# A streaming encoder layer with a product-key lookup beside it: stage barriers replaced by waits for producers, other paces, choices at other slots

## What is computed

```python
h = modulate(x, sh1, sc1)                       # layer norm, scale and shift from a vector c
gq, gk, gv, glr, gog, sq, sk, sv, mg_a, mg_b = split_cols(h @ w_in)
o_gla, s_fin = gla_recurrence(q, k, v, log_a, gla_s0)             # branch A, 4 heads
o_sb = stick_breaking(sbq, k_all, v_all, ...)                     # branch B, 16 heads of 64
mix = (sigmoid(mg_a) * branch_a + sigmoid(mg_b) * branch_b) @ w_o
x = layer_norm(DN_ALPHA * x + g1 * mix, ln1_w, ln1_b)
h2 = modulate(x, sh2, sc2)
# PEER: per token and head, the 16 best of 128 x 128 experts by two lists of 128 scores
sc, ix = lax.top_k(s, PEER_TOPK)
top, pos = lax.top_k(cand, PEER_TOPK)
g = softmax(top)
act = gelu(einsum('nhkd,nd->nhk', peer_u[eid], h2))
f = einsum('nhk,nhkd->nd', g * act, peer_v[eid])
x = layer_norm(DN_ALPHA * x + g2 * f, ln2_w, ln2_b)
```

## The kernel before

| stage | norm | stick | gla | mix | res | select |
|---|---|---|---|---|---|---|
| group 0, before and changed | 0 | 0 | 0 | 0 | 0 | 12 |
| group 1, before | 20 | 157 | 236 | 308 | 331 | 370 |
| group 1, changed | 15 | 168 | 243 | 311 | 333 | 370 |
| group 2, before | 378 | 551 | 626 | 695 | 717 | 754 |
| group 2, changed | 372 | 548 | 624 | 694 | 716 | 754 |

## Time and profile before

### The profile page before, as it was taken

One profiled execution on the slowest core, in us unless ns is written; L12 is line 12 of the kernel. 1 busy time (PEld: TensorE's weight loads), 2 busy tenths in 40 slices (PEclk: granted clock), 3 DMA queues, 4 the chain that ended last, 5 costly groups with the idle time before them and its releaser, 6 DMA issues.

```text
span 4522.3 us, 46382 instructions
## 1 busy us (share of the span) xinstructions
PE 3384.7 (75%) x16026; PEld 1667.0 (37%) x16026; DVE 2746.2 (61%) x6580; ACT 924.9 (20%) x1992; POOL 2407.8 (53%) x2375
## 2 busy tenths in 40 slices
PE   7988989878879989696899899798753433434355
PEld 4555755445536544253444356443320000000000
DVE  3343420689877864777776878655687676664420
ACT  3543210114432210013444523200100000000000
POOL 0000000134467756455877777655567777777776
PEclk9998999989989999898999999899865555555556
DMA  8774453478799999999999999999999999999998
GB/s 310 259 275 180 175 170 98 156 293 267 268 339 394 412 401 416 386 409 360 387 393 399 343 382 393 396 400 389 386 376 420 419 406 420 419 404 420 420 407 360
DMA packets 422694, 1572.17 MB, mean 348 GB/s; under 512 B 47720, under 2 KB 63464, under 8 KB 411328
## 3 DMA queue, kind: packets, MB, share of 16 engines
q0 software_dynamic: 340384, 1289.90, 72.6%
q1 hardware_dynamic: 78448, 271.38, 16.0%
...
...
## 4 chain that ended last, share of the span: by engine, by line
PE 44%; POOL 16%; DVE 16%; DMA 14%; issue 8%; ACT 2%; SPq 0%; ACTq 0%; DVEq 0%; POOLq 0%
PE wide L1847 8%; POOL peer_u_ring L2459 7%; DMA peer_v_ring<-in_peer_v,expertsT 6%; POOL peer_v_ring L2469 5%; PE bank L2526 5%; PE wide L2164 5%; DVE peer_u_ring L2632 4%; PE wide L1415 4%; POOL w_ring L2469 3%; PE wide L768 3%; DMA peer_u_ring<-in_peer_u,experts 3%; PE wide L1403 3%; PE bank L1847 2%; PE wide L831 2%; DMA w_ring<-in_peer_v,expertsT 2%
## 5 line engine op out<-in xcount | busy, mean ns | idle before, releaser
L2459 POOL DMA_INDIRECT peer_u_ring<-in_peer_u,experts x1098 | 1130.5, 1030 | 593.9 <-issue 287.5
L2632 DVE SCALAR_TENSOR_TENSOR peer_u_ring<-peer_u_ring,wide 128x1024 f32<-128x1024 f32 x682 | 821.3, 1217 | 560.1 <-DMA peer_u_ring<-in_peer_u,experts 541.7
L2469 POOL DMA_INDIRECT peer_v_ring<-in_peer_v,expertsT x840 | 880.6, 1048 | 478.1 <-PE bank L2526 254.5
L2526 PE MATMUL bank<-peer_v_ring,peer_lone 128*32 128x512 f32 x3360 | 559.4, 744 | 430.7 <-DMA peer_v_ring<-in_peer_v,expertsT 383.0
L2632 DVE SCALAR_TENSOR_TENSOR peer_u_ring<-peer_u_ring,peer_h 128x1024 f32<-128x1024 f32 x416 | 499.8, 1219 | 25.3 <-SPq L286 15.7
L2526 PE MATMUL bank<-w_ring,peer_lone 128*32 128x512 f32 x1056 | 249.9, 1035 | 348.1 <-DMA w_ring<-in_peer_v,expertsT 346.1
L2526 PEld LDWEIGHTS bank<-peer_v_ring,peer_lone 128*32 128x32 f32 x3360 | 78.2, 118 | 760.0 <-issue 712.9
L2469 POOL DMA_INDIRECT w_ring<-in_peer_v,expertsT x264 | 251.2, 951 | 84.4 <-issue 68.6
L2164 PE MATMUL wide<-mT,w_ring 128*128 128x384 f32 x768 | 266.3, 498 | 10.8 <-DMA w_ring<-in_weights 7.9
L768 PE MATMUL wide<-hT,w_ring 128*128 128x384 f32 x768 | 264.6, 491 | 6.1 <-DVE sb_hide L2746 3.1
L1415 PE MATMUL wide<-w_ring,hT 128*128 128x256 f32 x1152 | 263.8, 387 | 3.1 <-DVE gla_v L1741 3.1
...
## 6 DMA issues: line engine op xcount, KB each, us to landing
...
mod_w<-in_w_ada SPq DMA_DIRECT2D x15, 1024.0 KB, 11.1
...
```

The source lines that it names most:

```text
L2459: pool.indirect_dma_start(buffer, None, K.A["peer_u"], bass.IndirectOffsetOnAxis(ap=K.ids_of[:, j % CHOSEN, k:k + 1], axis=0)).then_inc(lo ...
L2469: pool.indirect_dma_start(buffer, None, K.A["peer_v"], bass.IndirectOffsetOnAxis(ap=K.ids_of_turned[:, j % CHOSEN, t:t + 1], axis=0)).then ...
L2526: last = pe.matmul(self.F.psum[strip:strip + 32, :], self.lone[:, mark - at:mark - at + 32], self.buffer("v", m)[0][:, c * HALF:(c + 1) * ...
L2632: dve.scalar_tensor_tensor(u, u, 1.0, h2, ALU.mult, ALU.mult, accum_out=self.dots[:, j % 2, k:k + 1]).then_inc(self.dot_done, 1)
```

## The change

`start` becomes `after`, which waits only for the engines that are named, and of those only PE and DVE report the end of a stage (`ended`). In nearly all places nothing is named, and waits for the very thing that is needed stand instead: PSUM banks kept, `mix.added` chunk by chunk, stores landed (`sequence_stored`, `outputs_stored`, `rows_stored`) on the engine that overwrites. SP waits for PE where it waited for all. POOL waits for the h2 rows and for PE's and DVE's ends.

The rows of x for the next group's norm go to a place of their own (`norm_x_behind`), are loaded in select and scaled there by DVE, between heads 2 to 5 of the choice (`scale_rows`, `more`). ACT takes the exponentials of the last two heads in the next norm and stick. Mix begins with the four chunks that need only `hT`, and `MIX_ORDER` orders the weights so. Res takes its eight weight chunks one by one.

In `paces` a slot of the first tile (s under 128) weighs `LONE_U` = 0.8 of another, and norm's units go from 10 to 3 for groups 1 and 2. The choice of a tile that is not a group's first begins 100 slots into the tile ahead of it, one head in every 12 slots, so that it ends 65 slots into its own tile; before it began 10 slots into the tile ahead (30 for tile 1, with 10 slots a head). Its ids are turned at slot 68 of its own tile, not 9. The h2 of the dots is read from PSUM in mix and res and in the tail, and from SBUF in norm and select too.

```diff
+LONE_U = 0.8
+MIX_ORDER = [(0, 0), (0, 1), (1, 0), (1, 1), (0, 2), (0, 3), (1, 2), (1, 3)] + [(j, m) for j in range(2, KC) for m in range(4)]
...
-    def start(self, e, G, name):
+    def after(self, e, G, name, *who):
...
         if at:
-            e.wait_ge(self.stage_done, 4 * at)
+            for w in who:
+                e.wait_ge(self.ended[w], at)
...
-    def end(self, e):
-        e.drain().then_inc(self.stage_done, 1)
+    def end(self, e, who):
+        e.drain().then_inc(self.ended[who], 1)
...
-        units += [10.0] * 2
+        units += [3.0 if g.n else 10.0] * 2
...
+        weights = [LONE_U if s < SLOTS else 1.0 for s in range(before, to)]
+        total, done, at, spent = sum(units[here:stop]), 0.0, before, 0.0
         for w in units[here:stop]:
             done += w
-            out.append(int(before + (to - before) * done / total))
+            while at < to and spent + weights[at - before] <= sum(weights) * done / total + 1e-6:
+                spent += weights[at - before]
+                at += 1
+            out.append(at)
...
+    def scale_rows(self, dve, G):
+        n, x = self.steps_before(G), self.x_of(G)
+        stats, mv, v, y, t = self.small_of(G)
+        for i in range(G.nt):
+            dve.wait_ge(self.x_in[i], 16 * sum(i < g.nt for g in GROUPS[:G.n + 1]))
+            for c in range(2):
+                dve.bn_stats(stats[:, i, c, :], x[:, i, c * HALF:(c + 1) * HALF]).then_inc(self.steps, 1)
+            dve.wait_ge(self.steps, n + 2)
+            dve.bn_aggr(mv[:, i, :], stats[:, i, :, :]).then_inc(self.steps, 1)
+            n += 3
+            yield
+        dve.wait_ge(self.steps, n)
+        n = rstd_steps(dve, self.steps, n, mv[:, 0:G.nt, 1], 1.0, LN_EPS, v[:, 0:G.nt], y[:, 0:G.nt], t[:, 0:G.nt])
+        dve.wait_ge(self.steps, n)
+        for i in range(G.nt):
+            dve.tensor_scalar(x[:, i, :], x[:, i, :], mv[:, i, 0:1], y[:, i:i + 1], ALU.subtract, ALU.mult).then_inc(self.ready, 1)
+        yield
...
         K.tick("PE", beside)
-        K.start(pe, G, "norm")
+        x = self.x_of(G)
...
-        K.end(act)
+        if G.n:
+            K.select.exp_best(act, GROUPS[G.n - 1].first, PEER_HEADS - 2)
...
+    def sequence_stored(self, e, G):
+        for b in range(2):
+            e.wait_ge(self.stored[b], 16 * (self.stores_before(G, b) + SB_PAIRS // 2 * self.stores(G)))
...
-        K.start(pe, G, "stick")
+        for k in range(KC - 4, KC):
+            pe.wait_ge(K.banks[k % 4].kept, K.banks[k % 4].at["norm", G.n, k])
...
+            act.wait_ge(K.select.sc_out, 16 * (K.select.after_choice(G.first - 1) + 1))
...
+            if n == 3 and G.n:
+                K.select.exp_best(act, GROUPS[G.n - 1].first, PEER_HEADS - 1)
...
-        K.start(pe, G, "gla")
         K.tick("PE", beside)
...
-        K.start(act, G, "gla")
+        K.stick.sequence_stored(act, G)
...
-        K.start(dve, G, "gla")
+        K.after(dve, G, "gla", "PE")
+        K.stick.sequence_stored(dve, G)
...
-        K.start(sp, G, "mix")
+        K.after(sp, G, "mix", "PE")
...
+        for c, (j, m) in enumerate(MIX_ORDER):
+            x = (K.hT, K.hT, self.oA, self.oB)[m]
...
+            w = K.chunk(pe, G, MIX_AT + c).rearrange("p (k n) -> p k n", k=KC)
+            if (j, m) == (0, 2):
+                pe.wait_ge(self.in_, 32 * (G.n + 1))
...
-        K.start(pe, G, "res")
-        w = [K.chunk(pe, G, RES_AT + n).rearrange("p (k n) -> p k n", k=2) for n in range(8)]
+        w = []
...
+                    if i == 0 and c == 0:
+                        pe.wait_ge(K.mix.added, KC * G.n + k + 1)
+                    if i == 0 and k % 2 == 0:
+                        w.append(K.chunk(pe, G, RES_AT + len(w)).rearrange("p (k n) -> p k n", k=2))
...
-    TURNS = ((30, 10, (0, 3, 5, 8), 7, (22, 61)),) + ((10, 12, (0, 3, 6, 9), 8, (3, 48)),) * (TILES - 1)
+    FROM, EVERY, STEPS_AT, EXP_AT, LOADS_AT = 100, 12, (0, 3, 6, 9), 8, (93, 138)
...
-        K.start(sp, G, "select")
+        K.after(sp, G, "select", "PE", "DVE")
         sp.dma_start(self.keysT[:, :, :], K.A["keysT"]).then_inc(self.const_in, 16)
...
+        if G.n + 1 < len(GROUPS):
+            K.res.rows_stored(sp, G)
+            K.norm.load(sp, GROUPS[G.n + 1])
...
-        K.start(pe, G, "select")
+        for c in range(2):
+            bank = K.res.y_bank(G.nt - 1, c)
+            pe.wait_ge(bank.kept, bank.at["h2", G.first + G.nt - 1, c])
...
-            if h:
+            if 0 < h < PEER_HEADS - 1:
                 self.exp_best(act, G.first, h - 1)
...
+        more = K.norm.scale_rows(dve, GROUPS[G.n + 1]) if G.n + 1 < len(GROUPS) else iter(())
...
+            if h >= 2:
+                next(more, None)
...
+        j, k = divmod(s - self.FROM, SLOTS)
+        if 0 <= j < TILES - 1 and self.chosen_beside(j + 1) and k < self.EVERY * PEER_HEADS:
+            return j + 1, k // self.EVERY, k % self.EVERY
...
-    IDS_AT = (18,) + (9,) * (TILES - 1)
+    IDS_AT = tuple(18 if j == 0 else 9 if j in [g.first for g in GROUPS] else 68 for j in range(TILES))
...
-        return self.K.dots_beside(s) not in ("stick", "gla")
+        return self.K.dots_beside(s) in ("mix", "res", None)
...
-                pool.wait_ge(K.stage_done, 4 * len(STAGES) * len(GROUPS))
+                pool.wait_ge(K.ended["PE"], len(STAGES) * len(GROUPS))
...
-            if j < TILES and k == self.IDS_AT[j] + 2:
+            if j < TILES and k == self.IDS_AT[j] + 1:
```

206 lines of the change are left out of this document (95 added, 111 removed).

## The result

The changed kernel takes 4503.4 us (4497.9 to 4504.8) beside 4529.0 for the kernel before on the same chip: ratio 0.9933, 95% interval 0.9918 to 0.9947. That is faster, but by 26 to 30 us and not by 84, and 4503 lies outside the range of 4400 to 4492. The profiled execution took 4504.4 us around a span of 4501.9. Of all executions in this document one, of exp_lone1_again, took 9451 us at a granted clock of 0.59 and is left out.

The account below looks back on a forecast made before the run. It took PE to bound the dense stages and gathers the tail. Terms summing to 84 us came off the profiled 4524.9 us, and 3.7 more for the median gave 4444.6 us; range 4400 to 4492.

Parts of the forecast that it names:

- Select's own starts: Two starts of select, where PE waits for a weight chunk: nothing won, 0 us, between -4 and +3.
- Rival B: PE waits at the ids' turn in the middle of six tiles: slower, 4557 us at 20 us each; chance 0.04.
- the pace: A first tile's slot at 0.8 moves 11 slots of group 1 ahead of stick's end: costed at nothing.
- my sum: All terms added over the whole kernel: 84 us saved, giving 4444.6 us; chance 0.52.
- barriers: PE's holes at stage ends go: 11 us won in group 0, 35 us in groups 1 and 2.
- the two norms: PE's idle time from select to the next norm shrinks: 22 us won before group 1, 20 us before group 2.
- clock: Ten holes fewer keep PE's granted clock up, 0.6 us each: 6 us won, ends 0 and 15.
- flow: Less slack between gathers and PE makes some landings late, 5% more waiting for v: 6 us lost.
- the second of what bounds the kernel: Room for gathers at 415 GB/s: groups 1 and 2 could lose 137 and 102 us before transfers alone hold them.
- The choices: Choices begun 100 slots into the tile ahead: 12 us won in sticks, 8 lost in mix and res, 8 at ids' turns.
- Res's -4 for each group: In res one head of 8.7 us stands ahead of a chain PE waits for: 4 us lost each time.
- Rival A: Transfers take back the barriers' gain as waits for v in groups 1 and 2: 45 us left, 4484; chance 0.15.

Follow-up runs that it names:

- exp_lone1_again: Second run of the changed kernel with the last two exponentials back in select and a first tile's slot at 1.0: ratio 0.9961.
- lone_1: The changed kernel with a first tile's slot at 1.0 instead of 0.8: 4539.8 us, ratio 1.0016.
- barriers_only: The changed kernel with choices at the old slots, a first tile's slot at 1.0 and the last two exponentials in select: 4507.7 us, ratio 0.9953.
- skip_exp: The changed kernel, last two exponentials in select, every second v gather from second tile to slot 754 replaced by a 1 KB transfer: 4411.0 us, ratio 0.9729.
- skip_before: The kernel before with every second v gather from the second tile to slot 754 replaced by a 1 KB transfer: 4495.1 us, ratio 0.9918.
- exp_in_select: The changed kernel with the exponentials of the last two heads of each group's first choice back in select: 4488.2 us, ratio 0.9904.
- skip24_exp: The changed kernel, last two exponentials in select, every second v gather left out from the 25th value to slot 754: 4542.5 us, ratio 0.9643.
- skip24_lone1: The changed kernel, exponentials in select, first tile's slot at 1.0, every second v gather left out from the 25th value: 4562.6 us, ratio 0.9690.
- holes_g2: exp_in_select with PE waiting again in group 2 for DVE's stage ends, stick's stores and oA and oB: 4505.2 us, ratio 0.9943.

## Why the prediction failed

*Where it held.* The gaps at the stage ends closed as written. In front of gla, mix and res of groups 1 and 2 they are 0.3 to 3.4 us, value pairs in them included; norm of group 1 starts at 949.1 right behind select (I wrote near 942; the slower first stick is 9 of it), the turn of the ids waits 2.9 us and stick 2.0, where I had left 6 and 2; norm of group 2 starts 19.4 us behind the last select matmul (17). Select's own starts kept 7.9 and 6.9 us. Rival B didn't come: no wait at an ids' turn is over 3 us, and the values behind it wait 4.3 at most. The tail took 1193 us, within 1185 to 1195.

*What was luck.* At norm of group 2 the program is 72 us ahead, which is near what my terms up to there come to (11, 22 and 20, and half of 35: some 70). But the pace, which I had at nothing, carries it: lone_1 is only 38 us ahead there and barriers_only 26. In the same way skip_exp is 84 us faster than skip_before, the very number of my sum, but some 20 of these are the pace. The terms for barriers, the two norms, clock and flow, 88 us together, gave 21 in barriers_only.

*The step that failed* is the second of what bounds the kernel: "groups 1 and 2 could lose 137 and 102 us before the transfers alone hold them". I compared the megabytes of a whole group with the 415 GB/s of the tail. In group 1 the average hid where the room was: in the stick, at a DMA share of 0.83. The 744 us behind it stood at 1.01 and 402 GB/s, and barriers_only, whose holes there shrank from 73 to 34 us, made them only 7 us shorter. In group 2 the share stood at 0.98 at 382 GB/s. Even at the 1.02 of the tail that leaves some 50 us and not 102 (an estimate from these rows), and none came: group 2 should have given some 15 us and took 44 (1242.3 to 1286.4). By the runs 25 of these are the late exponentials (exp_in_select), 14 the new places of the choices, and 5 are left for the replaced barriers (barriers_only). That it is room that was missing is shown by leaving gathers out: with the same cut exp_in_select's group 2 goes from 19 us longer than the kernel before's to 10 us shorter, and the distance of the two kernels from 45 to 84 us. The page "DMA: Bandwidth & Descriptors" of the Trainium skill, section "Specifications", with its 358 GB/s for a core, pointed the right way for the wrong reason: the trace holds 402 GB/s over 744 us of group 1, above that figure. Why a byte takes more engine time in group 2 than in the tail was not tried.

*The terms.* "A first tile's slot at 0.8: I cost it at nothing" failed in size: 37 us in the changed kernel and 0 in the kernel before. My sentence that it hides a lack of room for the shorter mix should have had a price, and it names the smaller part: with room for the transfers 20 us of the pace's worth stay (skip24_exp and skip24_lone1). The two exponentials moved behind norm and stick's third piece, which I counted only as a late turn of the ids, cost 25 us in group 2 and 13 in the time. Flow, -6, was -35 in group 2 alone (39.2 to 73.8 us of waits for v), 18 of them by the late exponentials. The choices, -4 in sum, were 0: more than the 12 us in the stick (376 to 346 us), and a cost behind it that I had too small. Res's -4 for each group was 4 to 6. The clock went the other way: 0.93 in group 2 for 0.95.

*Rival A* named the sign and the place, at 4484; with the exponentials in select 4488 was measured, and those two make 4503. But A took the transfers as a limit that what PE does cannot move, and it is not that: in the kernel before PE's path held group 2 (skip_before takes 249 gathers away for 38 us), and holes of 24 us in PE in exp_in_select still cost 17 us of time (holes_g2).
